# Expert weights in half fetches at both ends of the stream, a shorter router chain, the last combination by halves

## What is computed

```python
    grp = jnp.argmax(grp_logits, axis=-1)
    ...
    in_grp = jnp.take_along_axis(exp_logits, grp[:, None, None], axis=1)[:, 0]
    top_val, top_idx = lax.top_k(in_grp, MOE_TOP_K)
    gate = grp_p[:, None] * jax.nn.softmax(top_val, axis=-1)
    expert = grp[:, None] * MOE_EXPERTS_PER_GROUP + top_idx
    ...
    def run_block(args):
        xb, e = args
        hid = jax.nn.silu(xb @ w_gate[e]) * (xb @ w_up[e])
        return hid @ w_down[e]
```

## Time and profile before

| | |
|---|---|
| median of 3 runs | 966.71 us (965.07 to 967.89) |
| profiled execution | 966.98 us |
| its span | 965.1 us |
| TensorE busy | 908.6 us, 94% |
| VectorE, ScalarE, GpSimd busy | 279.2, 207.0, 196.6 us |
| DMA | 286.12 MB, mean 296 GB/s |
| mean granted clock | 0.996 |

### The profile page before, as it was taken

The page is one execution under the profiler, slowest core; times in us unless marked ns, Lnnn a source line. Parts: engine busy times, 40 slices in busy tenths (PEclk is TensorE's granted clock), DMA queues, the critical chain, the costliest instruction groups (busy, mean ns, idle before and its releaser), DMA issues.

```text
span 965.1 us, 13242 instructions
## 1 busy us (share of the span) xinstructions
PE 908.6 (94%) x5176; PEld 537.3 (56%) x5176; DVE 279.2 (29%) x738; ACT 207.0 (21%) x496; POOL 196.6 (20%) x327
## 2 busy tenths in 40 slices
PE   4999998999999999989889888999999999999996
PEld 3788686554443443434334334487766558688544
DVE  2399724310101111010010010134035336260334
ACT  2355514210000000000000000032215511011540
POOL 0187300121111111111011010032003201023221
PEclk9999999999999999999999999999999999999999
DMA  9997975689999999999999999991400934402001
GB/s 362 426 430 287 383 285 218 234 349 428 429 426 431 425 429 426 429 426 429 426 431 426 426 429 423 430 373 50 175 2 1 399 146 164 173 2 88 1 1 43
DMA packets 22522, 286.12 MB, mean 296 GB/s; under 512 B 2498, under 2 KB 3266, under 8 KB 4930
## 3 DMA queue, kind: packets, MB, share of 16 engines
q1 hardware_dynamic: 21744, 283.99, 70.9%
q10 hardware_dynamic: 722, 1.33, 0.4%
HBM read 284.26 MB, written 1.05 MB: 296 GB/s over the span
## 4 chain that ended last, share of the span: by engine, by line
PE 68%; DMA 20%; DVE 8%; issue 2%; POOL 1%; ACT 1%; SPq 0%; POOLq 0%; DVEq 0%; ACTq 0%
DMA arena<-in_w_expert_up 19%; PE bank L969 17%; PE bank L1205 16%; PE bank L1222 6%; DVE bank L1662 5%; PE bank L1415 5%; PE bank L1232 3%; PE bank L1362 3%; PE bank L1017 1%; PE bank L1193 1%; PE bank L1548 1%; PE bank L1394 1%; PE bank L1379 1%; PE bank L1446 1%; PE bank L1458 1%
## 5 line engine op out<-in xcount | busy, mean ns | idle before, releaser
L1205 PE MATMUL bank<-arena 128*64 128x512 f32 x1024 | 226.1, 594 | 24.0 <-DMA arena<-in_w_expert_up 24.0
L969 PE MATMUL bank<-arena 128*128 128x256 f32 (+1 forms) x992 | 211.1, 374 | 1.7 <-ACT arena L821 1.4
L969 PEld LDWEIGHTS bank<-arena 128*128 128x128 f32 x992 | 183.5, 190 | 27.9 <-issue 4.5
L1205 PEld LDWEIGHTS bank<-arena 128*64 128x64 f32 x1024 | 79.0, 137 | 167.2 <-issue 167.0
L1222 PE MATMUL bank<-arena 128*64 128x512 f32 x512 | 116.9, 599 | 0.8 <-ACT arena L791 0.8
L1862 DVE TENSOR_TENSOR arena<-bank,arena 64x512 f32<-64x512 f32 x32 | 21.8, 682 | 277.6 <-ACT arena L787 277.5
L791 ACT ACTIVATE arena<-bank 128x512 f32<-128x512 f32 x32 | 19.1, 597 | 386.1 <-PE bank L1214 386.1
L1222 PEld LDWEIGHTS bank<-arena 128*64 128x64 f32 x512 | 34.1, 136 | 65.8 <-issue 65.8
L550 POOL COPY der<-arena 128x4 f32 (+1 forms) x30 | 5.6, 187 | 318.4 <-PE bank L1214 298.4
L1232 PE MATMUL bank<-arena 64*128 64x256 f32 x512 | 65.8, 387 | 0.8 <-DVE arena L1865 0.8
L1662 DVE SCALAR_TENSOR_TENSOR bank<-arena,par,bank 128x256 f32<-128x256 f32 x143 | 58.3, 483 | 0.6
(11 more groups left out here) (252 smaller groups left out, 834.3 us busy)
## 6 DMA issues: line engine op xcount, KB each, us to landing
arena<-in_w_expert_down SPq DMA_DIRECT2D x32, 2048.0 KB, 31.6
arena<-in_w_expert_gate SPq DMA_DIRECT2D x31, 2048.0 KB, 25.9
arena<-in_w_expert_up SPq DMA_DIRECT2D x31, 2048.0 KB, 30.4
arena<-in_w_ada SPq DMA_DIRECT2D x12, 2048.0 KB, 31.0
arena<-in_w_kv SPq DMA_DIRECT2D x4, 2048.0 KB, 15.7
arena<-in_w_in_b SPq DMA_DIRECT2D x4, 2048.0 KB, 8.1
arena<-in_w_glu SPq DMA_DIRECT2D x3, 2048.0 KB, 36.2
arena<-in_w_uq SPq DMA_DIRECT2D x4, 1152.0 KB, 15.5
```

What stands on the lines that cost most here:

```text
L969: mm = pe.matmul(bank[part:part + m, at:at + n], w[:, k, lo:lo + m], rhs[:, k0 + k, :], start=(k == 0), stop=(k == tiles - 1))
L1205: mm = pe.matmul(GU_BANK[half * WIN:(half + 1) * WIN, :], xw[b][:, k, :], w[:, k, :], start=(k == 0), stop=(k == KD - 1), skip_group_check ...
```

## The change

It has three parts.

1. **Halves.** The gate and up matrices of experts 3, 4, 5, 29 and 30 are also fetched in halves. For 3, 4 and 5 SyncE issues the first halves when half of gate_up(0), (1), (2) is done, the second halves when all of it is. TensorE waits for the first halves before k = 0 and for the second before k = 4. In expert 31, the turn of 30 and the combination of 29 stand between the two halves of gate_up.
2. **Router.** `first_max` compares and multiplies in one instruction, against numbers less 64 (`iota_down`). One addition does both halves of the tokens. A Sqrt of a constant stands ahead of the last two squares. The ranks are summed in PSUM, the total counts have a bank of their own, and the weights come behind the selection. Of the four calls of `keep_busy` before the ranks one is left, and of the two behind them one.
3. **Last combination.** The copy and the combination of expert 31 are done in two halves, and the eight tiles are taken in the order 0, 1, 4, 5, 2, 3, 6, 7.

```diff
+COMBINED = (0, 1, 4, 5, 2, 3, 6, 7)
+HALVED = (3, 4, 5, 29, 30, 31)
...
+            def load_halves(e, b, lo):
+                for m in range(2):
+                    s = 3 * b + m
+                    src = expert_w[m][e:e + 1].rearrange("e p n -> p (e n)")
+                    sp.dma_start(arena[:, s * SLOT + lo:s * SLOT + lo + SLOT // 2], src[:, lo:lo + SLOT // 2]) \
+                        .then_inc(sem(f"slot{s}" if lo else f"upper{m}_{e}"), 16)
+
             def refill(e, b, freed_gate_up, freed_down):
 
-                sp.wait_ge(gu_full, freed_gate_up)
-                load_matrix(e + BODY, b, 0)
-                load_matrix(e + BODY, b, 1)
+                if isinstance(e, int) and e + BODY in HALVED:
+                    if e < BODY:
+                        sp.wait_ge(sem("gate_up_half"), e + 1)
+                        load_halves(e + BODY, b, 0)
+                        sp.wait_ge(gu_full, freed_gate_up)
+                        load_halves(e + BODY, b, SLOT // 2)
+                    else:
+                        sp.wait_ge(gu_full, freed_gate_up)
+                        load_halves(e + BODY, b, 0)
+                        load_halves(e + BODY, b, SLOT // 2)
+                else:
...
             for g in range(3):
+                if g == 2:
+                    act.activation(std_tok[:, 0:1], eps6, ACT.Sqrt)
                 for t in range(NT):
...
             bank = may_fill(pe, "rank")
-            keep_busy(bank, 4)
+            keep_busy(bank, 1)
...
-            pe.matmul(bank[:, 0:64], strict, both, start=True, stop=True)
-            pe.matmul(bank[:, 64:128], ones, both, start=True, stop=True).then_inc(full("rank"), 1)
+            picked = [small[:, 384 + EXPERTS * t:384 + EXPERTS * (t + 1)] for t in range(NT)]
+            pe.matmul(bank[:, 0:2 * EXPERTS], strict, small[:, 384:384 + 2 * EXPERTS], start=True, stop=False,
+                      skip_group_check=True)
+            pe.matmul(bank[:, EXPERTS:2 * EXPERTS], ones, picked[0], start=False, stop=True,
+                      skip_group_check=True).then_inc(full("rank"), 1)
+            bank = may_fill(pe, "count")
+            for t in range(NT):
+                mm = pe.matmul(bank[:, 0:EXPERTS], ones, picked[t], start=(t == 0), stop=(t == NT - 1))
...
-                    keep_busy(bank, 2)
+                    keep_busy(bank, 1)
...
-                gate_up(b, slot(3 * b + 1), slot(3 * b), ready).then_inc(gu_full, 1)
+                mm = gate_up(b, slot(3 * b + 1), slot(3 * b), ready, range(KD // 2))
+                if e < BODY:
+                    mm.then_inc(sem("gate_up_half"), 1)
+                if e == EXPERTS - 1:
+                    turn((b - 1) % BODY).then_inc(t_full, 1)
+                    pe.wait_ge(y_moved, e - 1)
+                    combine((b - 2) % BODY)
+                gate_up(b, slot(3 * b + 1), slot(3 * b), ready, range(KD // 2, KD)).then_inc(gu_full, 1)
...
+            pe.wait_ge(sem("last_y"), 1)
+            combine((EXPERTS - 1) % BODY, quarters=(0, 1)).then_inc(sem("combined_half"), 1)
             pe.wait_ge(y_moved, EXPERTS)
-            combine((EXPERTS - 1) % BODY).then_inc(sem("combined"), 1)
+            combine((EXPERTS - 1) % BODY, quarters=(2, 3)).then_inc(sem("combined"), 1)
...
+            dve.wait_ge(sem("route_in"), 16)
+            dve.tensor_scalar(iota_down, iota32, -2.0 * EXPERTS, None, ALU.add).then_inc(sem("iota_down"), 1)
...
                 then(dve.tensor_reduce(most, values, AX.X, ALU.max))
-                then(dve.tensor_tensor(flags, values, wide(most, n), ALU.is_equal))
                 for t in range(NT):
-                    ins = dve.scalar_tensor_tensor(out=cand[:, t, :], in0=flags[:, t, :], scalar=-64.0,
-                                                   in1=iota32[:, 0:n], op0=ALU.mult, op1=ALU.add)
+                    ins = dve.scalar_tensor_tensor(out=cand[:, t, :], in0=values[:, t, :], scalar=most[:, t:t + 1],
+                                                   in1=iota_down[:, 0:n], op0=ALU.is_equal, op1=ALU.mult)
...
-            for t in range(NT):
-                then(dve.tensor_tensor(em[:, t, :].rearrange("p (g e) -> p g e", g=GROUPS),
-                                       elog[:, t, :].rearrange("p (g e) -> p g e", g=GROUPS),
-                                       pen[:, t, :].unsqueeze(2).broadcast_to((P, GROUPS, PER_GROUP)), ALU.add))
+            then(dve.tensor_tensor(em.rearrange("p t (g e) -> p t g e", g=GROUPS),
+                                   elog.rearrange("p t (g e) -> p t g e", g=GROUPS),
+                                   pen.unsqueeze(3).broadcast_to((P, NT, GROUPS, PER_GROUP)), ALU.add))
...
-            dve.wait_ge(sem("group_exp"), 1)
-            gsum, gp, es, w1, w2 = (small[:, 520:522], small[:, 522:524], small[:, 524:526],
-                                    small[:, S_W1:S_W1 + 2], small[:, S_W2:S_W2 + 2])
-            then(dve.tensor_reduce(gsum, tmp(80, NT, 4), AX.X, ALU.add))
-            then(dve.reciprocal(gp, gsum))
-            dve.wait_ge(sem("pair_exp"), 1)
-            then(dve.tensor_scalar(es, small[:, 88:90], 1.0, None, ALU.add))
-            then(dve.reciprocal(es, es))
-            then(dve.tensor_tensor(w1, es, gp, ALU.mult))
-            then(dve.tensor_tensor(w2, w1, small[:, 88:90], ALU.mult))
...
-            dve.tensor_copy(counted, bank[:, 64:96]).then_inc(sem("ranks_step"), 1)
-            dve.tensor_copy(ranks[:, 0, :], bank[:, 0:32]).then_inc(sem("ranks_step"), 1)
-            dve.wait_ge(sem("ranks_step"), 1)
-            then(dve.tensor_tensor(ranks[:, 1, :], bank[:, 32:64], counted, ALU.add))
...
+            dve.wait_ge(sem("group_exp"), 1)
+            gsum, gp, es, w1, w2 = (small[:, 520:522], small[:, 522:524], small[:, 524:526],
+                                    small[:, S_W1:S_W1 + 2], small[:, S_W2:S_W2 + 2])
...
-            move_result(y_moved)
-            dve.wait_ge(sem("combined"), 1)
+            dve.tensor_copy(y_e[:, 0:T], Y_BANK[:, 0:T]).then_inc(sem("last_y"), 1)
+            dve.tensor_copy(y_e[:, T:2 * T], Y_BANK[:, T:2 * T]).then_inc(y_moved, 1)
...
-            for j in range(KD):
+            for j in COMBINED:
+                dve.wait_ge(sem("combined_half" if j in COMBINED[:4] else "combined"), 1)
```

More of the change, by code:

```diff
@@ L149, in two_blocks @@
         waste = area(R + 2048, NT, D)
+        iota_down = arena[:, R + 1792:R + 1792 + EXPERTS]
         xg = area(R, KD, PADDED)
@@ L456, in _ @@
                 refill(b, b, b + 1, b or None)
-            with sp.Fori(1, LOOPS - 1) as it:
+            with sp.Fori(1, LOOPS - 2) as it:
                 for b in range(BODY):
                     refill(it * BODY + b, b, it * BODY + (b + 1), it * BODY + b)
-            for b in range(PEELED - 1):
-                e = (LOOPS - 1) * BODY + b
-                refill(e, b, e + 1, e)
+            for e in range((LOOPS - 2) * BODY, EXPERTS - 1 - BODY):
+                refill(e, e % BODY, e + 1, e)
             last, b = EXPERTS - 1, PEELED - 1
             sp.wait_ge(gu_full, last - BODY + 1)
[L465 to L471, removed]
+            load_halves(last, b, 0)
+            load_halves(last, b, SLOT // 2)
             sp.wait_ge(y_full, last - BODY)
@@ L961, in total, with project @@
                 mm.then_inc(full(name), 1)
-            def project(name, w, lo, m, rhs, k0=0, n=T, at=0, part=0, tiles=KD, done=True, ready=None):
+            def project(name, w, lo, m, rhs, k0=0, n=T, at=0, part=0, tiles=KD, done=True, ready=None,
+                        order=range(KD)):
                 bank = ps[use[name][0]]
-                for k in range(tiles):
+                for i, k in enumerate(order[0:tiles]):
                     if ready:
-                        ready(k)
+                        ready(i)
                     mm = pe.matmul(bank[part:part + m, at:at + n], w[:, k, lo:lo + m], rhs[:, k0 + k, :],
-                                   start=(k == 0), stop=(k == tiles - 1))
+                                   start=(i == 0), stop=(i == tiles - 1))
                 if done:
@@ L1197, in _, with gate_up @@
             pe.wait_ge(sem("bank0_read"), BEFORE_EXPERTS[0])
-            def gate_up(b, wu, wg, ready=None):
-                for k in range(KD):
+            def gate_up(b, wu, wg, ready=None, ks=range(KD)):
+                for k in ks:
                     if ready:
@@ L1225, in down, with combine @@
                 return mm
-            def combine(b, first=False):
-                for j in range(4):
+            def combine(b, first=False, quarters=range(4)):
+                for j in quarters:
                     for half in range(2):
@@ L1733, in _ @@
             moved(dve, "shift_all")
-            dve.wait_ge(sem("route_in"), 16)
+            dve.wait_ge(sem("iota_down"), 1)
             logit = tmp(0, NT, CHOICES)
@@ L1813, in _ @@
             incl, start = small[:, 562:594], small[:, 594:626]
```

(5 more changed lines are left out.)

58 lines of the change are left out of this document (35 added, 23 removed).

## The result

| | before | changed kernel |
|---|---|---|
| median | 967.80 us (964.43 to 969.62, 9 runs) | 960.44 us (958.67 to 965.92, 9 runs) |
| profiled execution, its span | 966.98, 965.1 us | 965.92, 963.9 us |
| TensorE busy | 908.6 us | 912.2 us |
| mean granted clock | 0.996 | 0.995 |

The ratio is 0.9942, with a 95% interval of 0.9918 to 0.9966: faster, by 5.6 us. (The medians are 7.4 apart. The ratio goes with the means, 961.60 against 967.21, and so counts the long executions too. The gains given for the experiments are such ratios, times the median of the kernel before.) The forecast was 958.6, in a range of 956.8 to 961.6, that is a gain of 8.15.

A forecast was written before the change was run, and what follows sets the result against it. Bound by the router chain, then the experts' fetch stream with TensorE late at its end, then TensorE. Stream 4.0 plus lateness 2.8 plus last combination 1.35 make 8.15 off 966.98: 958.8, as a median 958.6; range 956.8 to 961.6.

The forecast's parts named there:

- TensorE's lateness: At the experts' end, TensorE starts down(30) after its matrix has landed; removing this delay gains 2.8 us.
- Last combination ... 1.35 gained: After the last expert, copying and combining by halves brings the first result 1.35 us sooner; bounds 1.0 to 1.4.
- The table load has no cover: In the router, loading the Sqrt table before the last two squares delays them; cost 0.5 us with the throw-away Sqrt.
- The weights moved behind the selection: Six router weight operations, 1.2 us, are covered by gate_up(0), 7 us long; uncovered they would cost 1.2.
- Rival B: At experts 29 and 30, halves do not land one by one; gain only 5.35 us, time 961.4; chance 0.07.
- E: In SyncE's fetch queue, each of ten added transfers costs 3.1 us; 22.9 net loss, time 990; chance 0.03.
- D: Late fetch issue gives back the start's gain; down(30) lands at its old time, leaving 1.35 and a part; chance 0.04.
- The router saves s = 1.5 us: The shorter router chain lets the first selection and later fetches come 1.5 us earlier; bounds 0.9 to 2.0.
- rival C: Fewer router fillers let TensorE's clock fall to half, costing 1.65 us; gain 6.5, time 960.2; chance 0.08.
- the price of the merged compare and multiply: In the router's first_max, merging saves 0.26 us in each of two wide calls, some 0.2 in the small one.
- a granted clock of 0.5 near 163: Sign of being wrong: TensorE at half clock around 163 us, in the router.
- 2.5 of the queue's gap: At the start, expert 5's halves follow without a gap, so the unbroken fetch stream comes 2.5 us earlier.

The follow-up runs named there:

- experiment 9: Kernel before, with experts 29 and 30 also halved and the turn and combination in the middle of 31; 963.77 us beside 966.13, ratio 0.9971.
- experiments 4: Changed kernel with the fillers of before and no Sqrt ahead of the last two squares; 959.90 us, ratio 0.9932.
- experiment 2: Changed kernel with the fillers of before (four products ahead of the ranks, two behind); 960.58 us, ratio 0.9939.
- experiment 5: Changed kernel with three fillers ahead of the ranks, one behind, no early Sqrt, experts 3 and 4 not halved; 959.77 us beside 966.26, ratio 0.9928.
- experiment 7: Kernel before with only experts 3, 4 and 5 newly halved (31 as before); 965.45 us beside 966.13, ratio 0.9989.
- experiment 1: The changed kernel run again without an edit; 959.86 us beside 966.74 for the kernel before, ratio 0.9938.
- experiment 6: As experiment 5, but with two fillers ahead of the ranks; 959.77 us, ratio 0.9933.

## Why the prediction was right, and where it was wrong

**What held.** The direction and the mechanisms of the three parts. The median lies in the range, but with some luck: 7 of the 19 executions lie above it, and of the forecast gain of 8.15 the ratios show 5.6 and 6.0. TensorE's lateness was forecast at 2.8: experiment 9 gave 2.8 us by its times, and in the change down(30) went from 3.1 behind its landing to 0.05. "Last combination ... 1.35 gained": 1.67 against 3.02 in the trace, though its own run resolves only 1.0. The table load has no cover: 0.5 forecast, 0.43 measured between experiments 4 and 2. The weights moved behind the selection cost nothing, since gate_up(0) follows the gather without a break. Rival B falls, the halves of expert 30 landed one by one, 2.4 to 2.6 apart; so does E, the ten added transfers left the stream at 427 GB/s; D would have shown as a down(30) landing late because of its issue, but in experiment 9 it was issued 3.8 later than before and landed at 613.3, as before (613.2).

**The step that failed** is "The router saves s = 1.5 us", and with it the chance of 0.08 for rival C. With the half clock the router saved nothing and lost 2.1 (19.15 against 17.06). At full clock it saves 1.2: the price of the merged compare and multiply was wrong. I took one whole step of VectorE out of each first_max and left the pair beside it at its old 0.31; but two merged instructions take 0.42 (L1787), so a wide call saves 0.15 and not 0.26. From the logits to the last selection it went from 5.30 us (157.78 to 163.08) to 4.66 (160.80 to 165.46): 0.64 where the text has 0.9. Behind the selection two errors nearly cancel: from the ranks to the gather it takes 1.59 (experiment 5), where the prediction's times give 1.25, and the gather itself is 0.27 shorter (3.57 against 3.84), which it did not have.

The rest is rival C. It was dismissed on a slice at 160 us in which TensorE was busy 0.08 of 1 us and kept a clock of 1.00. That slice was followed by two full ones, and says nothing of what comes a few us later: the trace of the change has a slice of 0.06 at 163 with a clock of 1.00, and the fall comes at 166. Nor was it rare: 7 of 19 executions of the change lie in the upper group. And the price was read from the wrong stretch: 3.3 us at half clock in the opening, "half of 3.3, 1.65". In the router it held from 166 to nearly 173, twice as long, over work that was all on the chain, and cost 3.3. If all seven long executions have it, it costs 1.2 in the mean. The prediction had named a granted clock of 0.5 near 163 as a sign of being wrong; the profile shows it 3 us later. The Trainium skill (TensorE: Matmul & The Clock Gate, Why this matters for your kernels) warns of idle gaps between bursts of matmuls. The runs bear out its direction, but TensorE's longest idle stretch in the profiled router was 1.42 us, with few products around it, and that row speaks of longer gaps. The prediction's "by that rule the fillers taken out are a loss" says more than the row does; the loss is what the runs show.

**A smaller miss** is "2.5 of the queue's gap". It gave 1.6 in the trace and 1.1 in the time (experiment 7), because the second halves of expert 5 did not follow the first without a break. Taken together: 8.15, less 0.3 for the router's steps, 0.7 for the queue's gap and 1.2 for the half clock in the mean, is 5.9, against 5.6 and 6.0 measured.

By themselves the parts gave 1.1, 2.8, 1.0 and 0.8 us, in sum 5.7. The lower group of the change stands 7.2 below the 966.74 that ran beside experiment 1, more than that sum; each part's interval is over 1 us wide to either side, so nothing follows from the difference.

**What may beat the change.** Experiment 5 has no execution above 960.21, where the change's 19 have a mean of 961.4: 1.6 us better in the mean, and 0.1 and 0.7 in the medians. The two were not run beside each other, so this rests on their ratios, 0.9928 (0.9911 to 0.9944) against 0.9942 and 0.9938, whose intervals overlap: likely, not shown. Against its own expectation of a gain from a shorter router it shows about 1 us less.

## What to carry to other kernels

Products that nobody reads may be what keeps TensorE's clock up while it waits: before taking some out, price the half clock over the work that follows, not over the gap, and look at all the times of the kernel, since the loss may come in one execution of three and hide from a median. Give the fillers just the length of the wait they fill: too many cost 0.5 us in each execution here (experiment 2), too few 3.3 in seven of 19. When an instruction is merged into another, take its time from a row of the same form, with its operands, or bound it by the sum of both. And where a part of a change is worth less than the scatter of the times, as three of the four are here, read it from the chain in a trace.

## What was not expected of the hardware

- **The issue of a fetch can block.** Near the end of the stream single issues of SyncE took up to 8.71 us (at 576.49, in the chain above), where each had taken 0.33 to 0.45 at the start (timeline of SyncE, changed kernel):

```profile
561.86 4.24 SPq L454 DMA_DIRECT2D arena<-in_w_expert_gate  x1
...
574.21 0.33 SPq L454 DMA_DIRECT2D arena<-in_w_expert_gate  x1
```

  The four halves of expert 30 and of 31 stand behind each other there, each landing some 30 us after its issue. It cost nothing that shows: the landings stayed 2.4 to 2.6 apart, and experiment 9 had it too. Before, with four halves instead of eight, no single issue there took over 0.43. It does put SyncE into the chain, and a kernel in which SyncE had other work to do there would feel it.
- **The clock falls elsewhere too.** Experiment 1's profile also shows 0.50 at 494 to 497 us, and experiment 6's at 486 to 489, in a stretch bound by the DMA. Eight of the fourteen traces have one such stretch, 3.4 us long, between 412 and 553 us, at places that differ from kernel to kernel. TensorE has slack there (it needs 13.0 of the 14.7 us of an expert), so it should cost nothing; no run tests that.
- **The table load's price.** It took 1.28 us, and the next activation began 0.02 later (159.33 behind 158.03 and 1.28). The Trainium skill (ScalarE: Activation LUTs, What ACT_TABLE_LOAD costs) gives 1283 ns for the load, which agrees, and 1380 ns for a drain beside it, which does not show here.
